# Gated linear attention: forget pair and values of two heads by seven products in three banks, levels by doubling

## The reference, cut to what matters

```python
q, f_fwd, f_bwd, i, z = split(h @ w_in)             # h: 512 latent + 256 context tokens
f = lb + (1 - lb) * sigmoid(f_pre);  k = 1 - f      # per direction and key column
q = silu(q);  v = i
# per direction, over chunks: b = cumsum(log f)
o = (q * exp(b)) @ S + sum_s<=t q_t . exp(b_t - b_s) k_s  v_s
S = exp(bL) * S + (k * exp(bL - b))^T @ v            # state, begun from the context
y = (rms(o_fwd + o_bwd) * silu(z)) @ w_out
```

## Time and profile before

| | us |
|---|---|
| median of three runs | 3677.27 |
| the profiled execution | 3675.11 |
| its span | 3673.3 |
| TensorE busy | 3558.3 |
| VectorE busy | 1997.6 |
| ScalarE busy | 1275.2 |
| GpSimd busy | 1026.7 |
| TensorE's granted clock, mean | 0.993 of full |

### The profile page before, as it was taken

The page is one execution under the profiler, slowest core; times in us unless marked ns, Lnnn a source line. Parts: engine busy times, 40 slices in busy tenths (PEclk is TensorE's granted clock), DMA queues, the critical chain, the costliest instruction groups (busy, mean ns, idle before and its releaser), DMA issues.

```text
span 3673.3 us, 54609 instructions
## 1 busy us (share of the span) xinstructions
PE 3558.3 (97%) x22490; PEld 2350.5 (64%) x22490; DVE 1997.6 (54%) x3490; ACT 1275.2 (35%) x2385; POOL 1026.7 (28%) x1008
## 2 busy tenths in 40 slices
PE   8999999999999999999999999999999999999998
PEld 4555555665668776776677757444455544878887
DVE  3555553445545425777777765354677742454543
ACT  3443443222231114444444531675445431010000
POOL 2212111222210004666666660222454430000000
PEclk9999999999999999999999999999999999999999
DMA  5121111100021121100111011222010111312221
GB/s 223 64 83 64 70 49 46 46 35 35 35 87 69 51 109 47 47 34 37 47 47 47 30 47 66 70 86 75 30 48 19 45 59 61 115 69 92 85 79 55
DMA packets 27255, 229.82 MB, mean 63 GB/s; under 512 B 2816, under 2 KB 6528, under 8 KB 9472
## 3 DMA queue, kind: packets, MB, share of 16 engines
q1 hardware_dynamic: 27008, 226.33, 16.5%
HBM read 224.22 MB, written 2.10 MB: 62 GB/s over the span
## 4 chain that ended last, share of the span: by engine, by line
PE 87%; DVE 6%; ACT 3%; issue 2%; POOL 1%; DMA 1%; SPq 0%; DVEq 0%; POOLq 0%; ACTq 0%
PE bank L1212 12%; PE bank L1505 9%; PE bank L1431 7%; PE bank L1849 7%; PE bank L1515 5%; PE bank L1876 4%; PE bank L1628 3%; PE bank L1495 3%; PE bank L1767 2%; PE bank L1337 2%; PE bank L1587 2%; PE bank L1594 2%; PE bank L1370 2%; PE bank L1159 2%; PE bank L1813 2%
## 5 line engine op out<-in xcount | busy, mean ns | idle before, releaser
L1505 PE MATMUL bank<-hT,ring 128*128 128x256 f32 (+1 forms) x1024 | 349.8, 490 | 0.0
L1212 PE MATMUL bank<-xT,ring 128*128 128x384 f32 x896 | 322.4, 493 | 2.5 <-ACT Y L1991 2.4
L1505 PEld LDWEIGHTS bank<-hT,ring 128*128 128x128 f32 x1024 | 189.6, 190 | 122.0 <-issue 108.1
L3488 POOL TENSOR_TENSOR ring<-ring 128x512 f32<-128x512 f32 x112 | 146.4, 1324 | 415.7 <-DMA ring<-in_w 414.0
L1212 PE MATMUL bank<-hT,ring 128*128 128x384 f32 x672 | 242.8, 493 | 0.0
L1212 PEld LDWEIGHTS bank<-xT,ring 128*128 128x128 f32 x896 | 160.7, 190 | 107.9 <-issue 14.1
L1628 PE MATMUL bank<-hT,ring 128*128 128x512 f32 x384 | 178.9, 600 | 4.8 <-ACT Y L1966 4.8
L1515 PE MATMUL bank<-ring,hT 128*128 128x128 f32 x1536 | 182.0, 277 | 0.0
L1515 PEld LDWEIGHTS bank<-ring,hT 128*128 128x128 f32 x1536 | 176.3, 192 | 2.1
L1212 PEld LDWEIGHTS bank<-hT,ring 128*128 128x128 f32 x672 | 121.4, 190 | 80.8 <-issue 16.0
L3651 POOL TENSOR_TENSOR hT<-hT,arena 128x512 f32<-128x512 f32 x3 | 5.1, 1723 | 558.6 <-ACT arena L1903 558.6
(11 more groups left out here) (589 smaller groups left out, 7719.6 us busy)
## 6 DMA issues: line engine op xcount, KB each, us to landing
ring<-in_w SPq DMA_DIRECT2D x51, 2048.0 KB, 8.4
ring<-in_w SPq DMA_DIRECT2D x45, 1024.0 KB, 4.8
ring<-in_w SPq DMA_DIRECT2D x20, 1280.0 KB, 5.5
ring<-in_w SPq DMA_DIRECT2D x10, 1536.0 KB, 7.3
ring<-in_w SPq DMA_DIRECT2D x8, 1408.0 KB, 6.0
ring<-in_w SPq DMA_DIRECT2D x6, 512.0 KB, 3.5
xT<-in_xT SPq DMA_DIRECT2D x1, 3072.0 KB, 14.7
xT<-in_xT SPq DMA_DIRECT2D x4, 512.0 KB, 6.5
```

Of the source, the lines that this page charges most:

```text
L1212: ins = e.matmul(bank[spot["st", kind, n, at]][:, 0:384], left[:, k], right[:, k], start=first and k == 0, stop=k == 3, skip_group_check=True)
L1505: ins = e.matmul(m[:, 0:b - a], w[:, k, sl(1 + d)], hT[:, k, a:b], start=k == 0, stop=k == 7)
L3488: e.tensor_tensor(s[:, i], l, r, op).then_inc(up("st_s", (kind, n, i)), 1)
```

## The change

- Two new kinds of slab replace the one of a head: `glf` (both forget gates of a head) and `glv` (values of two heads), 1 MB each, and `glq` (queries of two heads), 1 MB.
- `gs` computes the forget pair of a head, and the values of two heads, by seven products over 3 x 384 columns of PSUM in banks 0, 1 and 2. GpSimd makes four sums of weights a pair (`gs_s`) in the slot's upper half, VectorE four sums of tokens once (`gs_t`, during the gate projections before the stage), and the products are added on the way out by ScalarE (products 0 and 3) and VectorE (the others).
- The cumulative logs, their exponentials and the logarithm go. Queries and keys are multiplied up in place: from level to level the high block of each pair is multiplied by the total decay of the low block (VectorE), the low block's by that of the high block (GpSimd), and the totals of pairs are multiplied together (VectorE). Levels run from 1 to 64 tokens, were from 64 to 1. Below 32, ScalarE packs the keys (`gl_p`). The context keys get running products (`gl_c`: scans on VectorE, products on GpSimd).
- The turned keys are copied by VectorE. The jobs of a head are in another order: diagonal, levels, then transposes, states and output.
- `gl_steps` places work by estimated times (GL_TIME) rather than by counts.
- In layer 0, `na_vt` uses bank 7 - g.

```diff
+def gl_jobs():
     for j in range(16):
+        yield [[("gl_i", j), ("gl_d0", j), ("gl_c", j), ("gl_p", j, 0)], [("gl_d1", j), ("gl_m", j, 0)], [("gl_d2", j)]]
+        yield []
+        for li in range(1, 7):
+            yield [[("gl_x", j, li)] + [("gl_p", j, li)] * (li < 5) + [("gl_a", j, li - 1)], [("gl_m", j, li)]]
+        yield [[("gl_x", j, 7), ("gl_a", j, 6)]]
+        yield [[("gl_t", j, 0)], [("gl_u", j, 0)]]
+        yield [[("gl_t", j, 1)], [("gl_u", j, 1)], [("gl_o", j)], [("gl_n", j)], [("gl_y", j)]]
+GL_TIME = {"f": 1.29, "v": 1.39, "q": 1.72}
...
+def gl_queries(n):
+    made = [[("gl_q", j, c)] for j in (2 * n, 2 * n + 1) for c in range(4)]
+    made[5].append(("gl_qd", 2 * n))
+    made[7].append(("gl_qd", 2 * n + 1))
...
+        units = [("f", 0), ("q", 0)] if j < 0 else [("q", (j + 1) // 2), ("f", j + 1)] if j % 2 else [("v", j // 2), ("f", j + 1)]
...
             def na_vt(j, g):
-                m = take(7 if j else work, ("na_vt", j, g), ("na_v_turned", (j, g)))
+                m = take(7 - g if j else work, ("na_vt", j, g), ("na_v_turned", (j, g)))
...
+            def gs(kind, n, c):                      # TensorE; fourteen half products, c = 0 to 13
+                p, half = divmod(c, 2)
+                (g, u, sums), (h1, h2) = gs_factors(kind, n), ST_H
+                at, left, right, first = ((0, g[:, 0:4], hT[:, 0:4, h1], True), (1, sums[:, 1], gl_T[1], True),
+                                          (2, sums[:, 2], gl_T[2], True), (0, g[:, 4:8], hT[:, 4:8, h1], False),
+                                          (1, sums[:, 0], gl_T[0], True), (2, u[:, 4:8], gl_T[3], False),
+                                          (1, sums[:, 3], hT[:, 4:8, h2], False))[p]
...
+                if kind == "v":
+                    for i, k in [(i, k) for i in range(3) for k in range(4)][6 * half:6 * half + 6]:
+                        ins = e.matmul(m[:, sl(i)], right[:, k, sl(i)], left[:, k], start=first and i == k == 0, stop=k == 3,
+                                       skip_group_check=True)
+                else:
+                    for k in (2 * half, 2 * half + 1):
+                        ins = e.matmul(m[:, 0:384], left[:, k], right[:, k], start=first and k == 0, stop=k == 3,
+                                       skip_group_check=True)
...
             def gl_m(j, li):
+                m, size = take(work, ("gl_m", j, li), ("gl_a_level", (j, li))), 1 << li
+                q.wait_ge(*(on("gl_high", (j, li)) if li else on("gl_q_one", j)))
+                if li:
+                    q.wait_ge(*on("gl_low", (j, li)))
+                if size < 32:
+                    q.wait_ge(*on("gl_key_pack", (j, li)))
...
+            def gl_x(j, li):                         # VectorE: high halves, then totals
+                m = 1 << (li - 1)
+                q.wait_ge(*on("gl_m_mm", (j, li - 1)))
...
+                o = gl_half(j, HIGH_PART, m, 1)
+                e.tensor_tensor(o, o, gl_total(m, 0, m), ALU.mult).then_inc(up("gl_high", (j, li)), 1)
+                q.wait_ge(*on("gl_high", (j, li)))
+                q.wait_ge(*on("gl_low", (j, li)))
+                o = gl_D2.rearrange("p (d n) -> p d n", d=2) if m == 1 else gl_total(m, 1, 0)
+                e.tensor_tensor(o, gl_total(m, 0, 0), gl_total(m, 1, 0), ALU.mult).then_inc(up("gl_total", (j, li)), 1)
...
+            def gl_x(j, li):                         # GpSimd: low halves
+                m = 1 << (li - 1)
+                q.wait_ge(*on("gl_m_mm", (j, li - 1)))
...
+                o = gl_half(j, LOW_PART, m, 0)
+                e.tensor_tensor(o, o, gl_total(m, 1, m), ALU.mult).then_inc(up("gl_low", (j, li)), 1)
...
+            def gl_p(j, li):                         # ScalarE: pack keys of levels below 32
...
+                e.activation(gl_kp.rearrange("p (n h m) -> p n h m", n=n, h=2),
+                             gl_level(j, KEYS[0], KEYS[1], slice(0, LAT), 1 << li), ACT.Copy).then_inc(up("gl_key_pack", (j, li)), 1)
```

More of the change, by code:

```diff
@@ L342, in gl_steps @@
 def gl_steps():
[L343 to L357, removed]
+    made, filler, begins, at, late = [], [], [], 0.0, []
+    for j in range(-1, 15):
+        units = [("f", 0), ("q", 0)] if j < 0 else [("q", (j + 1) // 2), ("f", j + 1)] if j % 2 else [("v", j // 2), ("f", j + 1)]
+        if j >= 0:
+            begins.append(at)
+        for kind, n in units:
+            chunks = gl_queries(n) if kind == "q" else gs_pair(kind, n)
+            for at_, step in enumerate(late):
+                chunks[at_].append(step)
+            late = [("gl_g", n, 1), ("gl_g", n, 0)] if kind == "f" else []
+            for group in chunks:
+                filler.append((at, group))
+                at += GL_TIME[kind]
+    begins.append(at)
+    paired = [n for n, (_, group) in enumerate(filler) if group[0][0] == "gs" and group[0][3] == 0]
+    kinds = [filler[n][1][0][1:3] for n in paired]
+    for n, kind in zip(paired, kinds[1:]):
+        for i, step in enumerate(gs_sums(*kind)):
+            filler[n + 2 + 3 * i][1].append(step)
+    made += gs_sums("f", 0)
+    begins = [t + GL_LEAD for t in begins]
+    ticks = [begins[j] + i * (begins[j + 1] - begins[j]) / 11 for j in range(15) for i in range(11)]
+    heads = pipeline(gl_jobs())
+    filler = iter(filler)
+    t, group = next(filler)
+    for tick in ticks:
+        while group is not None and t <= tick:
+            made += group
+            t, group = next(filler, (0.0, None))
+        made += next(heads)
+    while group is not None:
+        made += group
+        t, group = next(filler, (0.0, None))
+    made += late
+    side = iter(gl_last())
+    for n, group in enumerate(heads):
+        made += group + next(side, []) + (next(side, []) if n < 11 and n % 3 else [])
     for group in side:
@@ L861, in ml_spread @@
             return (y[:, 14, :], y[:, 15, :]) if h < 3 else (ml_qk[:, 0, :], ml_qk[:, 1, :])
-        at[0], spare[0] = 0, 8192
+        at[0], spare[0] = 0, 14336
         lbm = place(64)
[L866 to L873, removed]
@@ L1509, in gl_v @@
[L1509 to L1519 removed]
+                    if j % 2:
+                        give("glq", "gl_q_mm", j)
@@ L1559, in gl_m @@
+                if size < 32:
+                    q.wait_ge(*on("gl_key_pack", (j, li)))
+                for kc, qc, p in squares_of(size):
+                    keys = gl_kp[:, kc] if size < 32 else gl_level(j, KEYS[0], KEYS[1], kc, size)
+                    ins = e.matmul(m[p, qc], keys, gl_level(j, QUERIES[1], QUERIES[0], qc, size), start=True, stop=True)
                 ins.then_inc(up("gl_m_mm", (j, li)), 1)
             def gl_o(j):
-                m, s4 = take(4, ("gl_o", j), ("gl_scaled", j)), gl_S[j % 2].rearrange("p (d c n) -> p d c n", d=2, c=4)
+                m, s4 = take(4, ("gl_o", j), ("gl_scaled", j)), gl_S.rearrange("p (d c n) -> p d c n", d=2, c=4)
@@ new lines, in gs_r @@
+            def gs_r(kind, n, p):
+                if p in (0, 3):
+                    return
+                m, (h1, h2) = bank[spot["gs", kind, n, {1: 1, 2: 2, 4: 1, 5: 2, 6: 1}[p]]][:, 0:384], ST_H
+                first, second = gs_tile(kind, n, 0), gs_tile(kind, n, 1)
+                q.wait_ge(*on("gs_mm", (kind, n, p)))
+                if p == 1:
+                    q.wait_ge(*on("gs_a", (kind, n, 0)))
+                elif p < 6:
+                    q.wait_ge(*on("gs_v", (kind, n, {2: 1, 4: 2, 5: 4}[p])))
+                o, other = {1: (first[:, h2], first[:, h1]), 2: (second[:, h2], first[:, h2]), 4: (second[:, h2], second[:, h2]),
+                            5: (second[:, h1], first[:, h2]), 6: (first[:, h2], first[:, h2])}[p]
+                e.tensor_tensor(o, m, other, ALU.add).then_inc(up("gs_v", (kind, n, p)), 1)
```

455 lines of the change are left out of this document (227 added, 228 removed).

## The result

The changed kernel takes 3655.12 us, the median of four runs (3652.86 to 3658.21), against 3677.15 us for the kernel before on the same chip (3672.29 to 3679.59). The ratio is 0.9942, 95% interval 0.9928 to 0.9955: 22 us faster, where 45.5 were forecast. The time is inside the range, the direction is right, and half the gain is missing.

A forecast was written before the change was run, and what follows sets the result against it. TensorE was taken to bound the kernel, full in the gated linear attention stage. 67 - 26 + 2.5 + 3 - 1 = 45.5 us less; 3675.1 - 45.5 + 2.2 = 3632 us, range of 8 in 10 3602 to 3668.

The forecast's parts named there:

- Work: Gated linear attention stage: TensorE loses 4.2 us of work a head, 67 us over 16 heads.
- Stalls: Gated linear attention stage: TensorE waits 3.5 us for two heads, 26 us over 15 heads; range 0 to 60.
- late slab, sum, low half: Even head: forget slab loads late, GpSimd's sum ahead of a low half waits for it; 1.0 us for two heads.
- queries' sigmoid and output before level 2: Odd head: VectorE waits for ScalarE passes, then query product and output precede level 2's high half; 2.1 us.
- three short gaps before packed levels: Three gaps of 2.7 us before packed levels: 0.1 to 0.2 us lost each, 0.4 together for two heads.
- The last head: End of the stage: the last head's 7.5 us of waits become about 5, 2.5 us gained.
- Layer 0: Neighbourhood attention stage: second group of turned values in bank 6 avoids waits for bank 7; 3 us gained, bounds 0 and 3.7.
- token sums: Four 128x1536 differences of context and latent halves on VectorE: 1 us lost, 8 if nothing covered them.
- B: Rival, chance 0.22: GpSimd's low halves take 2.2 us, 0.8 above the assumed 1.38; 22 us more, 3654 us.
- A: Rival, chance 0.18: nothing stalls, the order has slack enough and gains stay whole; 72.5 us less, 3605 us.
- C: Rival, chance 0.07: VectorE bounds each level, 4.8 us a level, 7.2 us of stalls a head; 36 us slower, 3713 us.
- D: Rival, chance 0.05: the change gives back what it saves, for example waiting on slab sums; about 3677 us.

The follow-up runs named there:

- e8: Changed kernel with four reorderings together: second decay scaling, sums of weights and odd head's query product later, fifth addition earlier; 3616.21 us, ratio 0.9834.
- e3: Changed kernel with GpSimd's sums of weights for the next pair placed two chunks later; 3644.68 us, ratio 0.9913.
- e7: Changed kernel with the odd head's query product (multiplication by the sigmoid) two chunks later; 3647.26 us, ratio 0.9919.
- e1: Changed kernel with the second decay scaling one chunk later, behind VectorE's copies of the turned keys; 3638.23 us, ratio 0.9898.
- e6: Changed kernel with VectorE's fifth addition of forget and value products ahead of the level's halves; 3642.76 us, ratio 0.9902.
- e10: Changed kernel with GpSimd's sums of weights made for only 8 of each 128 columns, the rest left out; 3630.93 us, ratio 0.9879.
- e9: e8 with filler (gate and output chunks) kept for the last head, extras at 3 ticks, not 7; 3605.13 us, ratio 0.9806.
- e4: Changed kernel with layer 0's second group of turned values in bank 7 again, as before the change; 3656.74 us, ratio 0.9948.
- e2: Changed kernel with the copies of the turned keys back on ScalarE; 3684.32 us, ratio 1.0018.
- e11: e8 with the copies of the turned keys on ScalarE; 3660.00 us, ratio 0.9957.

## Why the prediction was half right

**Work, right.** 67 us forecast, 62.6 found in the stage, and 64.3 when the half clock is set apart on both sides. In the middle of the stage the term stands: two heads went from 100.0 to 91.7 us of work (97.6 - 5.9), 66 us for sixteen heads, and e8 has 91.8 (92.4 - 0.55). The rest is at the ends of the stage and was not traced.

**Stalls, the step that failed.** The term was 26 us less 2.5 at the last head, 23.5 of waiting; the stage has 42.8 more than before. By place, for two heads:

| wait of TensorE | forecast | measured | shown by |
|---|---|---|---|
| late slab, sum, low half | 1.0 | 1.25 | e3: 10.4 us back |
| queries' sigmoid and output before level 2 | 2.1 | 0.9 | e7: 7.9 us back |
| three short gaps before packed levels | 0.4 | none seen | the timeline only |
| odd head's level 1, packing behind the norm's passes | 0 | 0.55 | the timeline only |
| state update for a copy of turned keys | 0 | 1.8 | e1: 16.9 us back |
| last forget product for the fifth addition | 0 | 1.4 | e6: 12.4 us back |

The places that the prediction named cost 2.15 us in place of 3.5. The largest of them was put too high because it took the output's last product and the high half at their long forms, 1.10 and 1.34 us; in the second stretch above both take 0.69. It missed three places, worth 3.7 us a pair. The two that matter gave back 29 us in e1 and e6, and each has one reason. The prediction counted VectorE's copies among the busy time and didn't ask what stands ahead of them in the queue: a scaling that waits for another engine. And it took the rule that VectorE and GpSimd hold each other for the two halves of a level alone, not for the totals behind them. There a product of eight elements costs 1.15 us, when a sum of weights runs beside it. The Trainium skill has the rule behind this (SBUF — State Buffer, section Who interferes with whom): a VectorE instruction with two SBUF inputs and a GpSimd one that reads SBUF exclude each other, and whichever starts first holds the shared ports for its whole instruction. The groups of e10 agree, 1.15 against 0.175 us.

**The last head, wrong in sign.** 2.5 us gained were forecast, but between the gate products 13 and 15 the stage takes 84.0 us (80.3 before, a stretch of half clock included), and 2.9 us of standing follow. The last head's waits are 8.0 us in five places, where 7.5 were to become 5. The filler that could have stood there was used up earlier:

```profile
2174.44 0.46 PE L1668 MATMUL bank<-arena 128*128 128x128 f32 x2 [1.63 <-DVE arena L3112]
...
2178.04 1.12 PE L1677 MATMUL bank<-arena,cons 128*128 128x512 f32 x2 [0.69 <-ACT arena L2327]
...
2182.11 5.40 PE L1549 MATMUL bank<-Y,ring 128*128 128x512 f32 x8 [2.95 <-DVE Y L3132]
```

The eight records of the last row take 5.40 us, most of it at half clock; the same eight at 2168.10 took 3.60. e9 moved filler there and got 11.1 us back, more than this tail shows, since e8's tail had a longer half clock.

**Layer 0, right.** 3 forecast, 2.4 read off the starts, and e4 brings back the row of seven waits. The term of 1 us for the token sums measures zero: the stretch that they lie in takes 777.9 us in both kernels.

**Rivals.** The time of B (3654) came out by coincidence, not B: its low halves of 2.2 us measure 1.41 us in the mean (1.06 to 1.80 in the middle of the stage), close to my 1.38. The rule named beside B (the Trainium skill, GPSIMD Engine Reference, section Performance pitfalls for Q7 kernels: half as much again for reads with a step over 8 bytes) doesn't show here. The shortest low half is 1.49 us at blocks of one, 1.27 at blocks of four and 1.06 at blocks of 64, so the long steps are not the dear ones. Nor is it a clean test of the rule, because the innermost step of that read is a repeat and the long step lies outside it. A is refuted as the change stands, since TensorE waits 36 of 710 us; yet its 3605 us is what e9 reaches, once the same instructions stand in another order. C, 7.2 us of stalls a head, did not come: there are 2.9, and VectorE was 67% busy where near 75% was forecast. Of its idea this much is true, that VectorE's queue sets the wait at the last forget product. D did not come.

**Where 22 us come from.** 62.6 less work, 42.8 more waiting and 2.4 in layer 0 make 22.2 us; the 2.6 us lost after the stage take the span's difference to 19.6, and the medians say 22. These two numbers, 19.6 from one execution and 22 from the medians, differ by no more than the runs scatter.

## What to carry to other kernels

When a change makes independent steps into a chain, walk each in-order queue at the busiest places and list what stands ahead of the step that the bounding engine waits for; above all a step that itself waits for a third engine and that nobody needs yet. Moving four kinds of step, with not an instruction changed, gave 39 us where the change itself had given 22. Keep filler work for the last round of a pipeline: four steps of it spent too early cost 11 us at the end.

## What the runs showed of the hardware

- A stand of 3.75 us of TensorE in an otherwise full stage went with 3.4 or 6.8 us at half clock, in each of the seven pairs of e2 and of e11. Moving two small copies to the engine with the most room cost 44 us that way in e11. A shorter wait is no safe one: of the changed kernel's eight waits of 1.6 to 2.0 us at line 1638 seven left the clock at full, and one did not. Its six records take 1.57 us in place of 0.94, and the window behind it (columns as above) has half clock:

```profile
1885.30 1.57 PE L1638 MATMUL bank<-arena,cons 128*128 128x128 f32 x6 [1.98 <-DVE cons L3050]
...
1885.50:1888.50 3.00, 3.00 (x15) 3.00 (x16) 0.67 (x3) 0.00 (x0) 0.00 (x0) 0.50 0.00 0
```

  The mean of the whole window still reads 1.00, because 3.4 us are too few to show in 710.
- A VectorE product with both inputs in SBUF can take 6.6 times as long (1151 against 175 ns) from a GpSimd sum alone; between 8 and 32 elements its size made no difference while it was held (1151 and 1180 ns). Freed of the sums, GpSimd's own low halves became no faster (1409 and 1527 ns).
